# The position bias of the differential pairs: 16-bit products on TensorE, or 32-bit additions on VectorE

## The chip, the cores and the metric

The kernel runs on one core of a Trainium2 chip. A core has TensorE (PE; matmuls, results to PSUM), VectorE (DVE), ScalarE (ACT), GpSimd (POOL) and SyncE (SP, which here only issues DMAs). Each engine takes its instructions strictly in the order in which the program lists them, and waits between engines are waits on counting semaphores. The metric is the time of one execution on the device in microseconds; for the kernel before, three runs took 2700.38, 2700.81 and 2706.25 us, median 2700.81 us.

## The reference

One layer of a hybrid encoder: a joint projection, eight forgetting-attention (FoX) heads, four differential heads, gates and an output projection. The change concerns the differential heads of the prompt (2048 tokens), cut to this:

```python
def diff_block(qp, q):
    s = jnp.einsum('bqhmd,bkhmd->bhmqk', q.astype(f32), kd) * SCALE      # m: two maps per head
    bias = table[t5_bucket(kpos[None, :] - qp[:, None])]
    s = s + jnp.transpose(bias, (2, 0, 1))[None, :, None]
    mask = (kpos[None, :] // CHUNK) <= (qp[:, None] // CHUNK)            # CHUNK = 64
    s = jnp.where(mask, s, NEG_INF)
    p = jax.nn.softmax(s, axis=-1)
    a = p[:, :, 0] - lam * p[:, :, 1]
    return jnp.einsum('bhqk,bkhe->bqhe', a, vd)
```

The bias depends on the distance of key and query alone and is constant from a distance of 128 on. Less that constant, which the softmax doesn't see, and with the mask put in, it differs from zero only in a band two key tiles wide beside the diagonal. The kernel keeps that band as a table of 128 x 256 per head, in two layouts (queries or keys along the partitions).

## The kernel before

Three parts follow each other: the projection of 2176 token columns with the attention of the sample rows woven in (to about 1400 us), the prompt's attention (to 2293 us), and the merge with the output projection. The prompt's attention (`prompt_attention`) goes over eight pairs: pair 0, 2, 4, 6 are two FoX heads each, pair 1, 3, 5, 7 are the two maps of a differential head. A pair has four blocks Q of 512 queries.

There are two passes. **Pass A** finds, for every query, the maximum of its scores and (differential pairs) the sum of the exponentials. A unit of it is one query tile of 128 against up to 1024 keys: TensorE writes the scores to one of two PSUM tiles `sa` (`scores_a`), VectorE takes the maximum (L1913), and for a differential pair ScalarE takes exponentials and their sum (L1861) before TensorE may write the unit after next. **Pass B** has 40 units per pair, one key tile against the 512 queries of a block: for each of two maps TensorE writes scores to `sb` (`scores_b`, one PSUM bank per map), ScalarE takes the exponential into `e` (L1891), VectorE combines the two maps into `w` (L1956; in FoX pairs it sums them up instead, L1972 and L1975), and TensorE multiplies by the values (`product`, L2070 or L2073). TensorE may not write the scores of the next unit to a bank before ScalarE has read this one's.

The bias enters by matmuls. In the projection part VectorE splits the 32-bit table into three bfloat16 parts (event B3, L728 to L738), and in both passes three matmuls of an identity with these parts (L2020 in pass A, L2047 in pass B) stand between the two score matmuls of a banded unit, in the same accumulation. Of pass B the key tiles 4Q-1 to 4Q+3 of a block are banded; of pass A one unit of most tiles.

The order of all this is one list of events written by `events()`; every engine walks it and emits its part. Around each unit u of pass B the list has B(u), E(u), W(u-1), R(u-2), then as many units of pass A (of the pair after, some nine units of pass B ahead) as a work target asks for, then the products V. So pass A of a differential pair runs mainly beside pass B of a FoX pair, and partly beside its own pass B.

## Time and profile before

| What | Value |
|---|---|
| median of three runs | 2700.81 us |
| the profiled execution | 2701.99 us, of which the span from first to last instruction is 2700.3 us |
| busy share of the span | PE 97%, PE weight loads 78%, DVE 49%, ACT 35%, POOL 14% |
| chain that ended last | PE 87%, ACT 4%, DVE 4%, issue 2%, DMA 2%, SPq 1%, POOL 1% |
| granted TensorE clock | 0.994 of full speed |

A row of a group names the line, the engine, the operation, the tiles and shapes, how many there are, the busy time with the mean length of one, and the idle time ahead of them with what ended it. Matmuls overlap in the records: a matmul's length runs from its start to the end of its results, and the next one starts before that, so what a matmul takes from the stream is read from one start to the next.

### The profile page before, as it was taken

To read this page: it belongs to the slowest core of one execution; us is meant where nothing else is said; L and a number is where in the kernel's file an instruction comes from. 1 tells how busy PE (TensorE), PEld (TensorE's weight loads), DVE (VectorE), ACT (ScalarE), POOL (GpSimd) and SP (SyncE) were. 2 spreads that over 40 slices of the span, in tenths; PEclk is the share of its full clock that TensorE was granted. 3 is DMA by queue.
4 is the path that set the end of the run, shared out by engine and by line. 5 is a ranking of instruction groups with operands and counts; after the bars stand their busy time and mean duration, and the time that the engine had idled before them with its cause. 6 is when DMAs were issued, how large, how long until landed. Compare 5 with 4: busy or idle time off the path is not lost.

```text
span 2700.3 us, 37170 instructions
## 1 busy us (share of the span) xinstructions
PE 2616.4 (97%) x14833; PEld 2100.3 (78%) x14833; DVE 1314.2 (49%) x1952; ACT 943.7 (35%) x1837; POOL 391.4 (14%) x398
## 2 busy tenths in 40 slices
PE   7999999999999999999999999999999999999998
PEld 5788888888999999999975565565566556888887
DVE  5321124314443332443347677667667766655553
ACT  4123321112222222100115655664664566422221
POOL 1100001131100000012244103212211330200000
PEclk9999999999999999999989999999999999999999
DMA  4543334448786676675843235054151422544432
GB/s 136 164 130 109 109 108 134 135 146 223 213 213 188 177 192 181 184 195 154 218 133 69 50 78 127 5 126 100 32 122 37 99 67 82 182 135 133 136 120 96
DMA packets 405772, 353.67 MB, mean 131 GB/s; under 512 B 45440, under 2 KB 368968, under 8 KB 399416
## 3 DMA queue, kind: packets, MB, share of 16 engines
q1 hardware_dynamic: 396464, 332.66, 45.6%
q0 software_dynamic: 9136, 18.63, 2.1%
...
## 4 chain that ended last, share of the span: by engine, by line
PE 87%; ACT 4%; DVE 4%; issue 2%; DMA 2%; SPq 1%; POOL 1%; ACTq 0%; DVEq 0%; POOLq 0%
PE p_acc L851 14%; PE p_acc L856 13%; PE p_acc L855 13%; PE a_op L2073 5%; PE a_sb L2042 4%; PE a_sb L2049 4%; PE a_op L2070 4%; PE a_sa L2018 3%; PE a_sa L2023 2%; PE e_U L1410 2%; PE a_sa L2021 2%; PE p_turn L885 2%; PE e_U L1411 2%; PE e_U L1412 2%; ACT a_e L1891 1%
## 5 line engine op out<-in xcount | busy, mean ns | idle before, releaser
L851 PE MATMUL p_acc<-p_h_hi,p_w_hi 128*128 128x384 f32 (+1 forms) x1960 | 718.0, 366 | 1.4 <-DVE p_h_lo L667 1.4
L856 PE MATMUL p_acc<-p_h_hi,p_w_lo 128*128 128x384 f32 (+1 forms) x1920 | 687.1, 358 | 0.0
L855 PE MATMUL p_acc<-p_h_lo,p_w_hi 128*128 128x384 f32 (+1 forms) x1920 | 686.5, 358 | 0.0
L1913 DVE TENSOR_REDUCE a_nmax<-a_sa 128x1 f32<-128x1024 f32 (+7 forms) x384 | 347.7, 910 | 282.2 <-PE a_sa L2021 166.7
L1891 ACT ACTIVATE a_e<-a_sb 128x512 f32<-128x512 f32 (+3 forms) x640 | 315.7, 534 | 313.7 <-PE a_sb L2049 311.2
L851 PEld LDWEIGHTS p_acc<-p_h_hi,p_w_hi 128*128 128x128 f32 x1960 | 369.7, 189 | 35.8 <-issue 4.0
L856 PEld LDWEIGHTS p_acc<-p_h_hi,p_w_lo 128*128 128x128 f32 x1920 | 361.0, 188 | 30.5
L855 PEld LDWEIGHTS p_acc<-p_h_lo,p_w_hi 128*128 128x128 f32 x1920 | 361.8, 188 | 28.7
L2042 PE MATMUL a_sb<-a_q,a_k 128*128 128x512 f32 (+2 forms) x640 | 276.5, 434 | 9.1 <-ACT a_e L1891 8.9
L2049 PE MATMUL a_sb<-a_q,a_k 68*128 68x512 f32 (+2 forms) x640 | 247.7, 389 | 0.0
L653 DVE TENSOR_TENSOR p_w_lo<-p_raw,p_w_hi 128x1024 fp32r<-128x1024 f32 x96 | 129.2, 1346 | 220.4 <-ACT p_w_hi L584 220.4
L564 POOL TENSOR_SCALAR p_ev_hi<-p_ev 128x896 fp32r<-128x896 f32 (+1 forms) x32 | 33.7, 1052 | 1234.3 <-DVE p_ev L551 1004.2
L584 ACT CAST p_w_hi<-p_raw 128x1024 fp32r<-128x1024 f32 x98 | 102.4, 1045 | 300.3 <-PE p_acc L856 254.6
L2042 PEld LDWEIGHTS a_sb<-a_q,a_k 128*128 128x128 f32 x640 | 122.7, 192 | 79.9 <-issue 35.0
L1861 ACT ACTIVATE a_sa<-a_sa,a_nmax 128x1024 f32<-128x1024 f32 (+4 forms) x192 | 162.6, 847 | 34.6 <-DVE a_nmax L1913 34.4
L551 DVE COPY p_ev<-p_acc 128x384 f32<-128x384 f32 (+1 forms) x80 | 48.8, 610 | 226.3 <-PE p_acc L856 226.3
L544 ACT ACTIVATE p_ev<-p_acc 128x384 f32<-128x384 f32 (+1 forms) x80 | 42.7, 534 | 298.9 <-PE p_acc L856 298.5
L2018 PE MATMUL a_sa<-a_k,a_q 128*128 128x512 f32 (+4 forms) x320 | 125.9, 394 | 20.6 <-ACT a_sa L1861 20.6
L2070 PE MATMUL a_op<-a_w,a_v 128*128 128x512 f32 (+3 forms) x320 | 144.8, 534 | 0.4
L2073 PE MATMUL a_op<-a_e,a_v 128*64 128x512 f32 (+3 forms) x640 | 139.0, 546 | 2.9 <-issue 2.9
L1975 DVE TENSOR_TENSOR a_run<-a_run,a_e 128x1024 f32<-128x1024 f32 (+3 forms) x128 | 137.4, 1074 | 1.4 <-DVE a_run L1975 0.5
L2049 PEld LDWEIGHTS a_sb<-a_q,a_k 68*128 68x128 f32 x640 | 122.5, 191 | 17.7 <-issue 5.5
...
## 6 DMA issues: line engine op xcount, KB each, us to landing
...
```

Of the source, the lines that this page charges most:

```text
L851: nc.tensor.matmul(acc[a % 2][:, 0:n], hi, h_hi[p][:, k, at:at + n], start=(k == 0), stop=False)
L855: nc.tensor.matmul(acc[a % 2][:, 0:n], hi, h_lo[p][:, k, at:at + n], start=False, stop=False)
L856: last = nc.tensor.matmul(acc[a % 2][:, 0:n], lo, h_hi[p][:, k, at:at + n], start=False, stop=(k == DK - 1))
L1861: nc.scalar.activation(scores_of(ev[1]), scores_of(ev[1]), ACT.Exp, bias=nmax[:, b % 2, c, col:col + 1], accum_out=total[:, b % 2, c, col: ...
L1891: nc.scalar.activation(e[:, u % E_SLOTS, m, cols], sb_[m][:, cols], ACT.Exp).then_inc(e_made, 1)
L1913: nc.vector.tensor_reduce(nmax[:, b % 2, c, col:col + 1], scores_of(ev[1]), axes, ALU.max, negate=True).then_inc(a_maxed, 1)
L1975: nc.vector.tensor_tensor(sum_, sum_, now, ALU.add).then_inc(e_added, 1)
L2018: nc.tensor.matmul(out, q1[z][m][:, qs], k1[z][m][:, k0:k0 + wide], start=True, stop=False)
L2042: nc.tensor.matmul(out, k1[z][m][:, ks], q1[z][m][:, qs], start=True, stop=False)
L2049: nc.tensor.matmul(out, k2[z][m][0:ROW_C + 2, ks], q2[z][m][0:ROW_C + 2, qs], start=False, stop=True).then_inc(b_scored, 1)
L2070: last = nc.tensor.matmul(op[:, cols], v[z][:, kt, :], w[:, u % W_SLOTS, cols], start=(kt == 0), stop=final)
L2073: last = nc.tensor.matmul(op[m * HD:(m + 1) * HD, cols], v[z][:, kt, m * HD:(m + 1) * HD], e[:, u % E_SLOTS, m, cols], start=(kt == 0), st ...
```

## The change

The three 16-bit parts go, with the VectorE work that makes them, and the band tables stay 32-bit. TensorE issues no bias matmuls any more. In pass A VectorE adds the table to the banded 128 or 256 columns of the scores in PSUM and then, waiting for its own addition (`a_biased`), takes the maximum. In pass B VectorE adds it to each map's scores in PSUM (`b_biased`); ScalarE's exponential of a banded unit waits for that addition instead of for TensorE. The addition stands at the event E(u), ahead of W(u-1) and of the maxima that follow it in the list. The table of a pair comes in two DMAs of 128 KB instead of six of 64 KB. The core of the diff:

```diff
@@ the projection part
-        for i in range(3):
-            at(10 + i, 0, ("B3", i))
+        at(10, 0, ("B3",))
@@ SyncE, B3
                 for y in range(2):
-                    sp.dma_start(d["band"][y, :, i].rearrange("h p n -> p h n"), part[i][:, y]).then_inc(band_stored, 16)
+                    sp.dma_start(d["band"][y].rearrange("h p n -> p h n"), band[:, y]).then_inc(band_stored, 16)
@@ VectorE, B3: the two memsets of the mask stay
-                    nc.vector.tensor_copy(part[0][:], band[:]).then_inc(band_step, 1)
-                    nc.vector.tensor_tensor(rest, band[:], part[0][:], ALU.subtract).then_inc(band_step, 1)
-                    nc.vector.tensor_copy(part[1][:], rest).then_inc(band_step, 1)
-                    nc.vector.tensor_tensor(rest, rest, part[1][:], ALU.subtract).then_inc(band_step, 1)
-                    nc.vector.tensor_copy(part[2][:], rest).then_inc(band_step, 1)
@@ prompt_attention
-        band = s.sb("band", [P, 2, 3, BAND], BF16)
+        band = s.sb("band", [P, 2, BAND])
+    def banded(a):
+        b, m, t, c = a
+        tile = 4 * (b % BLOCKS) + t
+        first = max((tile - 1) * P, c * CHUNK_KEYS)
+        end = c * CHUNK_KEYS + a_width(a)
+        return (end - first, first - (tile - 1) * P) if is_diff(b) and first < end else None
+    in_band = lambda b, kt: is_diff(b) and kt >= 4 * (b % BLOCKS) - 1
@@ ScalarE, E
-                    act.wait_ge(b_scored, 2 * u + m + 1)
+                    if in_band(*B_UNITS[u]):
+                        act.wait_ge(b_biased, 2 * n_band[u] + m + 1)
+                    else:
+                        act.wait_ge(b_scored, 2 * u + m + 1)
@@ VectorE, A
+                if banded(A_UNITS[ev[1]]):
+                    n, at = banded(A_UNITS[ev[1]])
+                    if (m, c) == (0, 0):
+                        dve.wait_ge(side_in[1], side_total(b // BLOCKS))
+                    b0, n_b = banks(a_width(A_UNITS[ev[1]]))[-1]
+                    end = n_b + (512 if b0 else 0)
+                    square = sa[ev[1] % 2][:, end - n:end]
+                    nc.vector.tensor_tensor(square, square, band[:, 0, at:at + n], ALU.add).then_inc(a_biased, 1)
+                    dve.wait_ge(a_biased, n_biased[ev[1] + 1])
@@ VectorE, E
+            elif ev[0] == "E" and in_band(*B_UNITS[ev[1]]):
+                u = ev[1]
+                t0 = B_UNITS[u][1] - 4 * (B_UNITS[u][0] % BLOCKS)
+                lo, hi = max(t0, 0) * P, min(t0 + 2, 4) * P
+                if t0 <= 0:
+                    dve.wait_ge(side_in[1], side_total(B_UNITS[u][0] // BLOCKS))
+                for m in range(MAPS):
+                    dve.wait_ge(b_scored, 2 * u + m + 1)
+                    nc.vector.tensor_tensor(sb_[m][:, lo:hi], sb_[m][:, lo:hi], band[:, 1, lo - t0 * P:hi - t0 * P],
+                                            ALU.add).then_inc(b_biased, 1)
@@ TensorE, scores_a
-                    for cols, msk in adds:
-                        nc.tensor.matmul(out[:, cols], ident16[:], msk, start=False, stop=False)
@@ TensorE, scores_b
-                if is_diff(b) and kt >= 4 * Q - 1:
-                    t0 = kt - 4 * Q
-                    lo, hi = max(t0, 0) * P, min(t0 + 2, 4) * P
-                    for n in range(3):
-                        nc.tensor.matmul(sb_[m][:, lo:hi], ident16[:], band[:, 1, n, lo - t0 * P:hi - t0 * P],
-                                         start=False, stop=False)
```

What moves on VectorE in pass B, at the end of the last block of pair 3 (about 1844 to 1853 us of the profile): `a_w` is the combined map, `a_nmax` the maximum of a pass A unit. Before:

```order
L1913 TENSOR_REDUCE a_nmax<-a_sa 128x1 [waits a_a_scored] x2
L1956 SCALAR_TENSOR_TENSOR a_w<-a_e,a_lam 128x512 [waits a_multiplied,a_e_made]
L1913 TENSOR_REDUCE a_nmax<-a_sa 128x1 [waits a_a_scored]
L1956 SCALAR_TENSOR_TENSOR a_w<-a_e,a_lam 128x512 [waits a_multiplied,a_e_made]
L1913 TENSOR_REDUCE a_nmax<-a_sa 128x1 [waits a_a_scored]
L1956 SCALAR_TENSOR_TENSOR a_w<-a_e,a_lam 128x384 [waits a_multiplied,a_e_made]
L1913 TENSOR_REDUCE a_nmax<-a_sa 128x1 [waits a_a_scored] x2
```

The same place in the changed kernel (its L1918 is L1913 of before, L1971 is L1956):

```order
L1918 TENSOR_REDUCE a_nmax<-a_sa 128x1 [waits a_a_scored] x2
L1964 TENSOR_TENSOR a_sb<-a_sb,a_band 128x256 [waits a_b_scored,a_side_in1]
L1964 TENSOR_TENSOR a_sb<-a_sb,a_band 128x256 [waits a_b_scored]
L1971 SCALAR_TENSOR_TENSOR a_w<-a_e,a_lam 128x512 [waits a_multiplied,a_e_made]
L1918 TENSOR_REDUCE a_nmax<-a_sa 128x1 [waits a_a_scored]
L1964 TENSOR_TENSOR a_sb<-a_sb,a_band 128x256 [waits a_b_scored] x2
L1971 SCALAR_TENSOR_TENSOR a_w<-a_e,a_lam 128x512 [waits a_multiplied,a_e_made]
L1918 TENSOR_REDUCE a_nmax<-a_sa 128x1 [waits a_a_scored]
L1964 TENSOR_TENSOR a_sb<-a_sb,a_band 128x256 [waits a_b_scored] x2
L1971 SCALAR_TENSOR_TENSOR a_w<-a_e,a_lam 128x384 [waits a_multiplied,a_e_made]
L1918 TENSOR_REDUCE a_nmax<-a_sa 128x1 [waits a_a_scored] x2
```

Two additions, each waiting for TensorE's scores of its map, now stand behind the maximum and ahead of the combination at every banded unit. What moves on VectorE in pass A of pair 3, beside pass B of pair 2 (`a_run` is the FoX sum, `a_const`, `a_c_hi` and `a_c_lo` close a block). Before:

```order
L1942 TENSOR_TENSOR a_const<-a_nmax,a_log_sum 128x8 [waits a_c_turned,a_f_act]
L1913 TENSOR_REDUCE a_nmax<-a_sa 128x1 [waits a_a_scored] x2
L1975 TENSOR_TENSOR a_run<-a_run,a_e 128x2x384 [waits a_e_added,a_e_masked,a_e_made]
L1948 CAST a_c_hi<-a_cT 8x128 [waits a_c_in1,a_c_turned]
L1950 TENSOR_TENSOR a_c_lo<-a_cT,a_c_hi 8x128 [waits a_f_dve]
L1913 TENSOR_REDUCE a_nmax<-a_sa 128x1 [waits a_a_scored]
L1975 TENSOR_TENSOR a_run<-a_run,a_e 128x2x256 [waits a_e_added,a_e_masked,a_e_made]
```

And after:

```order
L1947 TENSOR_TENSOR a_const<-a_nmax,a_log_sum 128x8 [waits a_c_turned,a_f_act]
L1915 TENSOR_TENSOR a_sa<-a_sa,a_band 128x256 [waits a_a_scored]
L1918 TENSOR_REDUCE a_nmax<-a_sa 128x1 [waits a_a_biased]
L1915 TENSOR_TENSOR a_sa<-a_sa,a_band 128x256 [waits a_side_in1,a_a_scored]
L1918 TENSOR_REDUCE a_nmax<-a_sa 128x1 [waits a_a_biased]
L1990 TENSOR_TENSOR a_run<-a_run,a_e 128x2x384 [waits a_e_added,a_e_masked,a_e_made]
L1953 CAST a_c_hi<-a_cT 8x128 [waits a_c_in1,a_c_turned]
L1955 TENSOR_TENSOR a_c_lo<-a_cT,a_c_hi 8x128 [waits a_f_dve]
L1915 TENSOR_TENSOR a_sa<-a_sa,a_band 128x256 [waits a_a_scored]
L1918 TENSOR_REDUCE a_nmax<-a_sa 128x1 [waits a_a_biased]
L1990 TENSOR_TENSOR a_run<-a_run,a_e 128x2x256 [waits a_e_added,a_e_masked,a_e_made]
```

Each banded maximum has an addition ahead of it, and waits for that addition; the order of everything else is as it was. On TensorE only the triples are gone.

## Rows read from the trace of the kernel before

**Rows 1.** The page: busy time, share of the span and instructions of each engine.

```profile
PE 2616.4 (97%) x14833; PEld 2100.3 (78%) x14833; DVE 1314.2 (49%) x1952; ACT 943.7 (35%) x1837; POOL 391.4 (14%) x398
```

**Rows 2.** Busy time by stretch: pass B of pair 2, of pair 3.

```profile
core 0: us, PE busy (x) PEld busy (x) DVE busy (x) ACT busy (x) POOL busy (x), PEclk, DMA share, GB/s
1633.00:1745.00 112.00, 105.86 (x523) 60.69 (x521) 80.96 (x95) 66.06 (x150) 35.77 (x43) 1.00 0.35 79
1745.00:1857.00 112.00, 109.76 (x552) 73.38 (x551) 75.96 (x120) 62.77 (x128) 13.56 (x22) 1.00 0.34 77
```

**Rows 3.** Groups by shape, 1350 to 2500 us: widest maximum, bias matmuls.

```profile
L1913 DVE TENSOR_REDUCE a_nmax<-a_sa 128x1 f32<-128x1024 f32 x160 | 195.6, 1223 | 146.0 <-PE a_sa L2021 82.3 <-PE a_sa L2023 51.4 <-PE a_sa L2025 12.2
...
L2020 PE MATMUL a_sa<-a_band,a_ident 128*128 128x256 bf16 x336 | 56.2, 276 | 0.0
L2047 PE MATMUL a_sb<-a_band,a_ident 128*128 128x256 bf16 x288 | 48.1, 276 | 0.0
L2047 PE MATMUL a_sb<-a_band,a_ident 128*128 128x128 bf16 x168 | 19.1, 223 | 0.0
...
L2020 PE MATMUL a_sa<-a_band,a_ident 128*128 128x128 bf16 x72 | 8.2, 223 | 0.0
```

**Rows 4.** Timeline of PE (start, length): map 1 without band, to the next start.

```profile
1600.63 0.40 PE L2042 MATMUL a_sb<-a_q,a_k 128*128 128x512 f32 x1
...
1601.10 1.02 PE L2070 MATMUL a_op<-a_w,a_v 128*128 128x512 f32 x2
```

**Rows 5.** Timeline of PE: map 1 of two banded units, to the next start.

```profile
1840.96 0.40 PE L2042 MATMUL a_sb<-a_q,a_k 128*128 128x512 f32 x1
...
1841.67 0.33 PE L2023 MATMUL a_sa<-a_k,a_q 66*128 66x384 f32 x1
...
1844.11 0.39 PE L2042 MATMUL a_sb<-a_q,a_k 128*128 128x512 f32 x1
...
1844.91 0.33 PE L2023 MATMUL a_sa<-a_k,a_q 66*128 66x384 f32 x1
```

**Rows 6.** Groups by shape, VectorE, whole span: the nearest operations.

```profile
L1913 DVE TENSOR_REDUCE a_nmax<-a_sa 128x1 f32<-128x256 f32 x32 | 13.0, 418 | 12.5 <-PE a_sa L2021 6.7 <-PE a_sa L2025 5.5
L1913 DVE TENSOR_REDUCE a_nmax<-a_sa 128x1 f32<-128x128 f32 x32 | 9.0, 286 | 15.5 <-PE a_sa L2021 9.8 <-PE a_sa L2025 5.6
...
L1343 DVE TENSOR_TENSOR e_pair<-e_pair,e_U 128x256 f32<-128x256 f32 x8 | 3.4, 421 | 9.9 <-PE e_U L1412 5.3 <-DMA e_pair<-scratch_gT 3.0 <-issue 1.5
```

**Rows 7.** Timeline of DVE: two maxima in a row, of 128 and of 256.

```profile
1575.14 0.54 DVE L1913 TENSOR_REDUCE a_nmax<-a_sa 128x1 f32<-128x128 f32 x2 [1.39 <-PE a_sa L2025]
...
1577.53 0.76 DVE L1913 TENSOR_REDUCE a_nmax<-a_sa 128x1 f32<-128x256 f32 x2 [0.46 <-PE a_sa L2025]
```

**Rows 8.** Busy time by stretch: the banded units of pair 3, blocks 3, 2, 1, 0.

```profile
1840.00:1853.00 13.00, 13.00 (x74) 8.04 (x73) 8.70 (x12) 4.61 (x10) 0.00 (x0) 1.00 0.00 0
1801.00:1814.00 13.00, 13.00 (x77) 8.05 (x75) 7.76 (x15) 4.26 (x9) 2.05 (x4) 1.00 0.01 2
1768.00:1783.00 15.00, 15.00 (x84) 9.90 (x82) 8.79 (x11) 9.41 (x18) 0.00 (x0) 1.00 1.02 213
1745.00:1759.00 14.00, 12.26 (x76) 7.92 (x75) 7.49 (x15) 8.90 (x21) 2.88 (x3) 1.00 0.01 2
```

**Rows 9.** Busy time by stretch: where VectorE is packed densest.

```profile
1649.00:1665.00 16.00, 15.22 (x77) 8.22 (x75) 13.98 (x15) 8.39 (x19) 4.58 (x6) 1.00 1.02 213
```

**Rows 10.** Waits, 1350 to 2600 us: total, times, longest.

```profile
PEld a_sa L2018 <- ACT a_sa L1861: 49.5, 60, 1.4
...
ACT a_sa L1861 <- DVE a_nmax L1913: 34.4, 44, 2.3
```

**Rows 11.** Busy time by stretch: where TensorE's granted clock is below full.

```profile
1390.00:1400.00 10.00, 6.54 (x18) 3.77 (x18) 7.10 (x10) 1.23 (x3) 5.29 (x4) 0.60 0.37 140
1400.00:1410.00 10.00, 7.10 (x24) 5.34 (x26) 5.04 (x8) 2.30 (x6) 9.42 (x9) 0.50 0.96 214
```

**Rows 12.** Busy time by stretch: projection, while B3 runs.

```profile
150.00:165.00 15.00, 15.00 (x68) 12.43 (x67) 5.41 (x6) 3.67 (x5) 0.00 (x0) 1.00 0.62 171
```

53 lines of the change are left out of this document (18 added, 35 removed).

## The prediction

> **What bounds the kernel now.** I read the page first: TensorE is busy 97% of the span, VectorE 49%, ScalarE 35% [rows 1]. A mean says little here, because the kernel has three parts, so I then cut the time into stretches. In the attention, pass B of a FoX pair and pass B of a differential pair alternate, 112 us each; pairs 2 and 3 stand for the others. In both TensorE is busy nearly throughout (105.9 and 109.8 of 112 us), while VectorE is busy 81.0 and 76.0 of 112 us [rows 2]: 72% and 68%, not 49%. So TensorE bounds both, and VectorE has some 31 to 36 us to spare in each. The groups by shape give what the change removes, the timelines what one piece of it takes, and the waits where a unit already hangs on another engine.
>
> **What it takes from TensorE.** 336 + 72 bias matmuls in pass A and 288 + 168 in pass B [rows 3]: 112 triples of 256 columns and 24 of 128 in pass A, 96 and 56 in pass B. Their busy time is 56.2 + 8.2 + 48.1 + 19.1 = 131.6 us [rows 3], but records overlap, so I measure from start to start. One map without a band takes 1601.10 - 1600.63 = 0.47 us [rows 4]. With a triple of 256 it takes 1844.91 - 1844.11 = 0.80, with one of 128 1841.67 - 1840.96 = 0.71 us [rows 5]. A triple is worth 0.33 or 0.24 us. Pass A: 112 x 0.33 + 24 x 0.24 = 42.7 us. Pass B: 96 x 0.33 + 56 x 0.24 = 45.1 us. Together 87.8 us, if TensorE alone decided.
>
> The Trainium skill says in "Perfetto Trace Analysis", section "Identifying the Most-Contended Engine", that busy time of matmuls is no good measure, since they are pipelined. By the busy column one would expect 131.6 us; the trace agrees with the rule, since the starts leave 87.8 of them.
>
> **What it adds to VectorE.** 136 additions in pass A, 152 in pass B, 208 of 256 columns and 80 of 128. The trace has no addition that reads and writes PSUM. The nearest are an addition of 256 columns with one operand in PSUM, 0.421 us, and the maxima over PSUM of 256 and 128 columns, 0.418 and 0.286 us [rows 6]. Two maxima in a row take 0.76 and 0.54 us together [rows 7], so the second adds only 0.34 or 0.25 us. I take these as what an addition takes from VectorE where nothing waits for it, and 0.42 (0.29) plus 0.03 for the hand-over as what it puts into a chain. The lower end is the same 0.34. For the upper end I let a write to PSUM double the length, 0.84 us: nothing in the rows speaks for that, and it is the end of the range, not the value.
>
> **Pass B, by stretch.** A stretch is the four or five banded units that end a block. The four of pair 3 last 14, 15, 13 and 13 us with VectorE busy 7.5, 8.8, 7.8 and 8.7 us [rows 8]. Block 0 has 6 triples of 256 and 2 of 128, 2.5 us of TensorE and, as additions, 6 x 0.34 + 2 x 0.25 = 2.5 us of VectorE. The others have 6 and 4, 2.9 and 3.0 us. TensorE would need 11.5, 12.1, 10.1 and 10.1 us, VectorE 10.0, 11.8, 10.8 and 11.7. So TensorE still decides in blocks 0 and 1, and VectorE takes over in blocks 2 and 3. Were VectorE packed without a gap, the stretches would take 11.5, 12.1, 10.8 and 11.7 us: 2.5 + 2.9 + 2.2 + 1.3 = 8.9 us per pair, 35.6 us over four pairs. It won't be. Its order is fixed and it waits for each map's scores, with the combination and the maxima behind it. The densest stretch in the trace has it busy 13.98 of 16 us, 87% [rows 9]. At 87% they would take 11.5, 13.6, 12.4 and 13.4 us: 2.5 + 1.4 + 0.6 - 0.4 = 4.1 us per pair, 16.4 us in all. I take the middle, 26 us of the 45.1.
>
> Beside it stands a rule that speaks against the change. The Trainium skill ("Perfetto Trace Analysis", "Optimizing Scalar/DVE Operations") gives VectorE an overhead of about 125 ns per instruction on PSUM. With 128 more columns costing 0.418 - 0.286 = 0.132 us, 256 columns are 0.264 us, and an estimate by that page is 0.39 us of engine time instead of 0.34. That adds 0.4 us to each stretch that VectorE bounds and takes some 3 us from the 26. The two maxima in a row are PSUM reads and cost 0.34 [rows 7], so the trace does not bear it out for reads; for a write to PSUM no row decides.
>
> **Pass A.** VectorE has room here: pass A of a differential pair lies mostly beside pass B of a FoX pair, 81.0 us busy of 112 [rows 2], and 25 additions of about 0.4 make it 91 of about 104. What matters is the loop of one `sa` tile: scores, addition, maximum, exponential, and only then the scores of the unit after next. The loop loses a triple (-0.33) and gains an addition with its hand-over (+0.45): +0.12 us. Where TensorE sets the pace the triple is a gain; where the loop does, it becomes +0.12, 0.45 us less than that. TensorE's weight load waits for this exponential 60 times, and the exponential itself waits for the maximum 44 times in all [rows 10]. In the others ScalarE was busy with pass B exponentials, which cover the addition. I count the 44: 42.7 - 44 x 0.45 = 22.9 us. The ends are 42.7 us (all covered) and, with all 136 on the loop, -136 x 0.12 = -16 us.
>
> **Edits at nothing.** The splitting of the table and its stores go, in a stretch where TensorE is busy 15.00 of 15 us [rows 12]: it hides them, and nothing is gained. Four stores and sixteen loads of the table fewer are no term: their issue on SyncE stands beside hundreds of others, and no wait of rows 10 is on them. ScalarE keeps its instructions; its exponential of a banded unit comes later by an addition and earlier by the triples ahead of its scores, 0.42 against 0.33 for map 0.
>
> **Sum.** 26 + 22.9 = 49 us, taken from the profiled execution's 2701.99 us (its span and 1.7 us around it, 1.2 us over the median): 2653 us.
>
> **Rivals.**
> 1. *TensorE stays the bound, VectorE hides everything.* For it: the 31 to 36 us to spare per stretch of 112 [rows 2], against about 10 us of additions in a FoX stretch and 15 in a differential one. Against it: blocks 2 and 3 [rows 8], where demand exceeds TensorE's. Time 2701.99 - 87.8 = 2614 us; whatever ends below 2635 I count here.
> 2. *The gain is lost to hand-overs.* Pass B gives its 16 us, pass A nothing, or the additions run long: at 0.84 us, 0.5 us more each, a stretch of blocks 2 and 3 grows by 5 us and eats that up. Time 2685 to 2706 us.
> 3. *Slower: the addition queues behind a maximum.* A maximum of 1024 columns takes 1.22 us [rows 3], and VectorE is strictly in order, so map 0's scores lie until it ends, ScalarE's exponential and TensorE's next scores behind them. At half a maximum plus the addition, 0.6 + 0.34, all 76 banded units could wait up to 0.95 us. It decides from 45.1 / 76 = 0.59 us of TensorE wait per unit. At the full 0.95 pass B turns from -45 to +27 us, and with pass A at nothing the time is 2729 us. For it: the order puts the maxima directly ahead of the additions. Against it: TensorE has a pass A unit's scores and a product, whose two matmuls alone are 1.02 us long [rows 4], to do in between, and two `sa` tiles of lead.
> 4. *The clock.* Where TensorE was busy only 6.5 and 7.1 of 10 us, the granted clock was 0.60 and 0.50, that is partly and wholly at 1.2 of its 2.4 GHz [rows 11]; in all stretches of rows 2 and 8 it was full. With VectorE as bound TensorE would be busy about 10.1 of 12.4 us, 81%, well above. If it fell in the eight stretches of blocks 2 and 3, each would need 10.1 us more: 80 us, 2734 us.
>
> **How the numbers follow.** The forecast (2635 to 2680) 0.52, rival 1 0.20, rival 2 0.17, rival 3 0.09, rival 4 0.02. A change under 0.2%, 5.4 us, can't be told from none: 2695.4 to 2706.2 us. Of rival 2 I put 0.09 on faster, 0.06 on the same, 0.02 on slower. Faster 0.52 + 0.20 + 0.09 = 0.81, same 0.06, slower 0.02 + 0.09 + 0.02 = 0.13. The range leaves out the complete cover, below 2620, and what lies above 2702: 2620 to 2702 us.
>
> **What the profile will show.** PE loses 864 matmuls, and the FoX and differential stretches fall from 112 us, together by about 12 us per pair of pairs: more by far than that means rival 1, and less rival 2. Additions in PSUM should read 0.42 and 0.29 us; 0.6 or more would break the sum in pass B first. In blocks 2 and 3 of pair 3 VectorE should be busy over 85% and TensorE wait for ScalarE's exponential, in blocks 0 and 1 not. In pass A ScalarE's waits for a maximum should become more than 44. The forecast is wrong if the exponential of banded units starts more than 0.6 us later after its scores than an addition takes, unit after unit, or if the clock falls anywhere past 1420 us.

## The result: a third of the gain that was forecast

| | before | after |
|---|---|---|
| median | 2700.86 us (4 runs, 2700.38 to 2706.25) | 2683.68 us (4 runs, 2682.77 to 2686.19) |
| ratio | | 0.993, 95% interval 0.9918 to 0.9943 |
| profiled execution / span | 2701.99 / 2700.3 us | 2683.03 / 2681.3 us |
| granted TensorE clock | 0.994 | 0.986 |

The change gains 17 us, and the forecast was 49 (2653 us). The sign and the range (2620 to 2702 us) held, the size did not.

### The profile page after: what moved, and what is told of

Same layout as the page of the kernel before. It is cut to its first block, busy times and chain, and to the rows that moved or that the text cites. A ratio compares the mean times of both kernels' runs of the same rounds, so it can differ in the third digit from the quotient of the medians.

```text
span 2681.3 us, 35769 instructions
## 1 busy us (share of the span) xinstructions
PE 2560.4 (95%) x13969; PEld 2055.5 (77%) x13969; DVE 1396.2 (52%) x2235; ACT 939.4 (35%) x1837; POOL 392.6 (15%) x398
## 4 chain that ended last, share of the span: by engine, by line
PE 81%; DVE 7%; ACT 5%; issue 3%; DMA 2%; SPq 1%; POOL 1%; DVEq 0%; ACTq 0%; POOLq 0%
PE p_acc L832 14%; PE p_acc L837 14%; PE p_acc L836 14%; PE a_op L2074 5%; PE a_sb L2049 4%; PE a_sb L2050 3%; PE a_op L2071 3%; PE a_sa L2027 2%; PE a_sa L2030 2%; PE e_U L1391 2%; PE p_turn L866 2%; PE e_U L1392 2%; PE e_U L1393 2%; ACT a_e L1887 2%; PE a_sa L2028 2%
## 5 line engine op out<-in xcount | busy, mean ns | idle before, releaser
L1918 DVE TENSOR_REDUCE a_nmax<-a_sa 128x1 f32<-128x1024 f32 (+7 forms) x384 | 347.0, 910 | 130.1 <-PE a_sa L2032 43.9
L1887 ACT ACTIVATE a_e<-a_sb 128x512 f32<-128x512 f32 (+3 forms) x640 | 310.6, 533 | 281.7 <-PE a_sb L2050 185.2
L2049 PE MATMUL a_sb<-a_q,a_k 128*128 128x512 f32 (+2 forms) x640 | 277.0, 436 | 21.1 <-ACT a_e L1887 18.1
L2050 PE MATMUL a_sb<-a_q,a_k 68*128 68x512 f32 (+2 forms) x640 | 237.5, 374 | 0.0
L2049 PEld LDWEIGHTS a_sb<-a_q,a_k 128*128 128x128 f32 x640 | 124.3, 194 | 109.3 <-ACT a_e L1887 52.1
L579 ACT CAST p_w_hi<-p_raw 128x1024 fp32r<-128x1024 f32 x98 | 102.4, 1045 | 300.0 <-PE p_acc L837 241.6
L1854 ACT ACTIVATE a_sa<-a_sa,a_nmax 128x1024 f32<-128x1024 f32 (+4 forms) x192 | 162.3, 846 | 50.8 <-DVE a_nmax L1918 49.6
L2027 PE MATMUL a_sa<-a_k,a_q 128*128 128x512 f32 (+4 forms) x320 | 132.0, 414 | 41.0 <-ACT a_sa L1854 40.9
L539 ACT ACTIVATE p_ev<-p_acc 128x384 f32<-128x384 f32 (+1 forms) x80 | 42.7, 534 | 298.5 <-PE p_acc L837 298.1
L2074 PE MATMUL a_op<-a_e,a_v 128*64 128x512 f32 (+3 forms) x640 | 144.5, 565 | 2.9 <-issue 2.9
L2050 PEld LDWEIGHTS a_sb<-a_q,a_k 68*128 68x128 f32 x640 | 124.7, 195 | 23.2 <-issue 10.1
L1990 DVE TENSOR_TENSOR a_run<-a_run,a_e 128x1024 f32<-128x1024 f32 (+3 forms) x128 | 137.1, 1071 | 0.6
```

The source lines that it names most:

```text
L1854: nc.scalar.activation(scores_of(ev[1]), scores_of(ev[1]), ACT.Exp, bias=nmax[:, b % 2, c, col:col + 1], accum_out=total[:, b % 2, c, col: ...
L1887: nc.scalar.activation(e[:, u % E_SLOTS, m, cols], sb_[m][:, cols], ACT.Exp).then_inc(e_made, 1)
L1918: nc.vector.tensor_reduce(nmax[:, b % 2, c, col:col + 1], scores_of(ev[1]), axes, ALU.max, negate=True).then_inc(a_maxed, 1)
L1990: nc.vector.tensor_tensor(sum_, sum_, now, ALU.add).then_inc(e_added, 1)
L2027: nc.tensor.matmul(out, q1[z][m][:, qs], k1[z][m][:, k0:k0 + wide], start=True, stop=False)
L2049: nc.tensor.matmul(out, k1[z][m][:, ks], q1[z][m][:, qs], start=True, stop=False)
```

## The profile after

The page after, answering [rows 1]: busy time, share of the span and instructions of each engine.

```profile
PE 2560.4 (95%) x13969; PEld 2055.5 (77%) x13969; DVE 1396.2 (52%) x2235; ACT 939.4 (35%) x1837; POOL 392.6 (15%) x398
```

The 864 matmuls are gone, VectorE has 283 instructions and 82 us more. Pass B of pair 2 and of pair 3 after, answering [rows 2]:

```profile
core 0: us, PE busy (x) PEld busy (x) DVE busy (x) ACT busy (x) POOL busy (x), PEclk, DMA share, GB/s
1627.50:1737.50 110.00, 100.63 (x441) 55.86 (x439) 88.40 (x119) 65.56 (x148) 35.40 (x42) 0.97 0.36 80
1737.50:1841.50 104.00, 95.91 (x391) 63.16 (x390) 87.58 (x163) 59.39 (x124) 12.99 (x20) 0.98 0.37 82
```

TensorE now stands idle 9.4 and 8.1 us in them, against 6.1 and 2.2 before, and its clock is no longer full. VectorE is at 80% and 84%, so over the whole stretch its busy time bounds neither. How long the stretches are is read best from the products of the differential pairs, by their line: durations (min, median, max) and first and last start, in pair 1, pair 3 and pair 7. Before:

```profile
L2070 PE MATMUL a_op<-a_w,a_v x80: 272/591/667, 1531.9 to 1632.2; 128*128 128x512 f32 x56, 128*128 128x384 f32 x8, 128*128 128x256 f32 x8, 128*128 128x128 f32 x8
L2070 PE MATMUL a_op<-a_w,a_v x80: 272/590/667, 1756.1 to 1856.3; 128*128 128x512 f32 x56, 128*128 128x384 f32 x8, 128*128 128x256 f32 x8, 128*128 128x128 f32 x8
L2070 PE MATMUL a_op<-a_w,a_v x80: 272/590/594, 2204.2 to 2292.6; 128*128 128x512 f32 x56, 128*128 128x384 f32 x8, 128*128 128x256 f32 x8, 128*128 128x128 f32 x8
```

And after:

```profile
L2071 PE MATMUL a_op<-a_w,a_v x80: 272/592/668, 1530.5 to 1625.5; 128*128 128x512 f32 x56, 128*128 128x384 f32 x8, 128*128 128x256 f32 x8, 128*128 128x128 f32 x8
L2071 PE MATMUL a_op<-a_w,a_v x80: 272/592/1191, 1749.2 to 1844.5; 128*128 128x512 f32 x56, 128*128 128x384 f32 x8, 128*128 128x256 f32 x8, 128*128 128x128 f32 x8
L2071 PE MATMUL a_op<-a_w,a_v x80: 272/590/1055, 2186.1 to 2274.3; 128*128 128x512 f32 x56, 128*128 128x384 f32 x8, 128*128 128x256 f32 x8, 128*128 128x128 f32 x8
```

From pair 1 to pair 3 a pair of pairs takes 218.7 us instead of 224.2; 12 us less was forecast (the same distance from pair 3 to 5 and from pair 5 to 7 shrank by 3.9 and 7.3 us). The differential part of pair 3 (first to last product) went from 100.2 to 95.3 us, the part ahead of it, from the last differential product of pair 1 on, below called a FoX stretch, from 123.9 to 123.7. Some 8 of the 10.7 us of TensorE work that pass A loses per pair lay there, and no gain is to be seen. The stretch also holds most of block 0 of the differential pair: its scores begin at 1737.7, its first product at 1749.2.

The last differential part, pair 7, gained nothing worth the name: 88.4 us before, 88.2 after, where pairs 1, 3 and 5 gained 5.3, 4.9 and 5.5. The longest pause of TensorE there is before block 3, for a DMA that brings the row constants made from pass A's maxima:

```profile
2241.40 0.50 PE L2049 MATMUL a_sb<-a_q,a_k 128*128 128x512 f32 x1 [2.75 <-DMA a_q<-a_c_lo]
```

In the trace of before TensorE's matmuls don't wait for this DMA at all; one weight load does, for 0.7 us.

The additions and the widest maximum by shape (after; the maximum is L1918 now), answering [rows 3, 6]:

```profile
L1918 DVE TENSOR_REDUCE a_nmax<-a_sa 128x1 f32<-128x1024 f32 x160 | 195.4, 1222 | 93.7 <-PE a_sa L2030 42.8 <-PE a_sa L2028 37.5 <-PE a_sa L2032 12.2
L1915 DVE TENSOR_TENSOR a_sa<-a_sa,a_band 128x256 f32<-128x256 f32 x112 | 47.7, 426 | 34.1 <-PE a_sa L2028 33.6
L1964 DVE TENSOR_TENSOR a_sb<-a_sb,a_band 128x256 f32<-128x256 f32 x96 | 37.5, 424 | 6.5 <-PE a_sb L2050 6.1
L1964 DVE TENSOR_TENSOR a_sb<-a_sb,a_band 128x128 f32<-128x128 f32 x56 | 14.9, 292 | 4.0 <-PE a_sb L2050 2.3
```

The price of an addition that reads and writes PSUM was forecast well: 0.42 and 0.29 us, and the double length at the end of the range did not come. The waits, answering [rows 10]. Before, beside the weight loads of those rows, the matmuls themselves waited this long:

```profile
PE a_sa L2018 <- ACT a_sa L1861: 20.6, 36, 1.2
```

After; exponentials are L1854 in pass A, L1887 in pass B, scores L2027 and L2049:

```profile
ACT a_e L1887 <- DVE a_sb L1964: 94.7, 72, 3.7
PEld a_sa L2027 <- ACT a_sa L1854: 76.3, 83, 2.3
PEld a_sb L2049 <- ACT a_e L1887: 52.1, 123, 1.8
ACT a_sa L1854 <- DVE a_nmax L1918: 49.6, 53, 2.4
PE a_sa L2027 <- ACT a_sa L1854: 40.9, 49, 1.9
```

TensorE's weight load waits for the pass A exponential 83 times and 76.3 us, against 60 times and 49.5 us, and the matmul 40.9 us against 20.6; the exponential for its maximum 53 times against 44. So a good part of the time went into the loop of the `sa` tile, and it is ScalarE's exponential that TensorE waits for.

How such a pause comes about, in pass B of pair 2: VectorE's timeline (start, length, idle time before), then ScalarE's, then TensorE's.

```profile
1708.52 1.22 DVE L1918 TENSOR_REDUCE a_nmax<-a_sa 128x1 f32<-128x1024 f32 x1
```

```profile
1707.77 0.19 ACT L1854 ACTIVATION_READ_ACCUMULATOR a_sa<-a_sa,a_nmax 128x1 f32 x1
1710.37 1.08 ACT L1887 ACTIVATE a_e<-a_sb 128x512 f32<-128x512 f32 x2 [2.40 <-PE a_sb L2050]
1711.34 1.10 ACT L1854 ACTIVATE a_sa<-a_sa,a_nmax 128x1024 f32<-128x1024 f32 x1
```

```profile
1710.64 0.29 PE L2027 MATMUL a_sa<-a_k,a_q 128*128 128x256 f32 x1
...
1712.60 0.50 PE L2027 MATMUL a_sa<-a_k,a_q 128*128 128x512 f32 x1 [1.55 <-ACT a_sa L1854]
...
1714.02 0.63 PE L2049 MATMUL a_sb<-a_q,a_k 128*128 128x512 f32 x1
1714.44 0.63 PE L2050 MATMUL a_sb<-a_q,a_k 68*128 68x512 f32 x1
...
1716.28 3.68 PE L2074 MATMUL a_op<-a_e,a_v 128*64 128x512 f32 x8
...
1719.90 0.52 PE L2049 MATMUL a_sb<-a_q,a_k 128*128 128x512 f32 x1
```

VectorE ended the maximum of this 1024-wide unit at 1708.52 + 1.22 = 1709.74. ScalarE, idle, did not take its exponential then: in its order two pass B exponentials stand ahead, whose scores came at 1710.4. So it began at 1711.34, ended at 1712.4, and TensorE stood 1.55 us. Then a second cost shows: matmuls of 512 columns start 0.42 us apart (1714.02, 1714.44) instead of 0.23. The granted clock fell to 1.2 GHz (0.66 as a mean of 1710 to 1720 us, shown below). The same place of pair 6 had the same pause without the fall:

```profile
2151.24 0.50 PE L2027 MATMUL a_sa<-a_k,a_q 128*128 128x512 f32 x1 [1.55 <-ACT a_sa L1854]
...
2152.29 0.39 PE L2049 MATMUL a_sb<-a_q,a_k 128*128 128x512 f32 x1
2152.52 0.40 PE L2050 MATMUL a_sb<-a_q,a_k 68*128 68x512 f32 x1
...
2153.55 1.94 PE L2074 MATMUL a_op<-a_e,a_v 128*64 128x512 f32 x8
2155.42 0.50 PE L2049 MATMUL a_sb<-a_q,a_k 128*128 128x512 f32 x1
```

From scores to the next scores it is 1719.90 - 1714.02 = 5.88 us there and 2155.42 - 2152.29 = 3.13 us here: 2.75 us from this fall in one unit. Three of the stretches with such falls, answering [rows 11]; past 1420 us the trace of before had none in the attention:

```profile
core 0: us, PE busy (x) PEld busy (x) DVE busy (x) ACT busy (x) POOL busy (x), PEclk, DMA share, GB/s
1710.00:1720.00 10.00, 8.45 (x25) 4.37 (x23) 5.99 (x8) 4.93 (x10) 0.00 (x0) 0.66 0.00 0
1740.00:1750.00 10.00, 6.62 (x29) 4.52 (x30) 6.00 (x15) 6.16 (x15) 0.86 (x1) 0.86 0.00 1
2180.00:2190.00 10.00, 8.91 (x34) 5.40 (x31) 5.77 (x13) 5.93 (x14) 3.85 (x4) 0.62 0.00 1
```

The trace has seven falls in the attention. The pause of TensorE last before each was 1.1, 1.6, 2.1, 1.6, 1.9, 1.9 and 2.75 us long; the last one is the wait for the DMA of pair 7. Of the other six, three lie in FoX pairs and three in block 0 of pairs 3, 5 and 7.

The four banded stretches of pair 3, from the start of the first unit's scores to the start of the next stretch (forecast at 87% packing and in full):

| us | block 0 | block 1 | block 2 | block 3 |
|---|---|---|---|---|
| before | 15.70 | 17.12 | 13.86 | 13.11 |
| after | 16.23 | 15.06 | 11.47 | 12.37 |
| gain | -0.53 | 2.06 | 2.39 | 0.74 |
| forecast gain | 2.5 | 1.4 to 2.9 | 0.6 to 2.2 | -0.4 to 1.3 |

Blocks 1 to 3 came as forecast. VectorE is busy 11.26 of 11.47 us in block 2 and 11.84 of 12.37 in block 3, 98% and 96%: it is the bound there, as the forecast had it, and packed closer than the 87% of its lower end. Block 0, where I let TensorE decide, got slower. VectorE there, after:

```profile
1742.48 1.23 DVE L1918 TENSOR_REDUCE a_nmax<-a_sa 128x1 f32<-128x1024 f32 x1 [1.45 <-PE a_sa L2028]
...
1743.98 0.76 DVE L1964 TENSOR_TENSOR a_sb<-a_sb,a_band 128x256 f32<-128x256 f32 x2
1744.64 0.74 DVE L1971 SCALAR_TENSOR_TENSOR a_w<-a_e,a_lam 128x512 f32<-128x512 f32 x1
1745.30 0.42 DVE L1990 TENSOR_TENSOR a_run<-a_run,a_e 128x256 f32<-128x256 f32 x1
```

And TensorE beside it:

```profile
1743.07 0.65 PE L2074 MATMUL a_op<-a_e,a_v 128*64 128x256 f32 x4
1745.87 1.08 PE L2099 MATMUL a_cT<-a_run,a_ones 128*64 128x512 f32 x4 [2.14 <-DVE a_gap L1932]
```

Block 0 of a differential pair is where the FoX pair ahead of it is closed. The matmul that totals that pair's sums (L2099) needs its last sum (L1990), and on VectorE this stands behind a maximum, two additions and a combination: TensorE waits 2.14 us, against 0.78 before. The releaser named, L1932, comes right behind the sum. Some 4.6 us earlier in the same block TensorE waits for a pass A exponential, 1.87 us against 0.96 before.

The row of two additions at 1743.98 also settles what I left open beside the Trainium skill ("Perfetto Trace Analysis", "Optimizing Scalar/DVE Operations"): two take 0.76 us, so the second adds 0.34 us, as two maxima did. The estimate of 0.39 us from that page's overhead on PSUM is not borne out for a write to PSUM either.

## The experiments

The kernel before took 2701 to 2702 us beside every group of them, so differences of a microsecond or two between groups mean nothing. Low time below is 2 x (1 - granted clock) x span: the kernel before has 32 us (0.994), the changed one 75 us (0.986).

**One pass each.** In `b_only` VectorE adds in pass B and TensorE keeps pass A's triples; `a_only` is the reverse. The edit of `b_only` against the changed kernel:

```diff
@@ VectorE, A
-                    nc.vector.tensor_tensor(square, square, band[:, 0, at:at + n], ALU.add).then_inc(a_biased, 1)
@@ TensorE, scores_a
+                        adds += [(slice(at, at + n_m), band[:, n, c0:c0 + n_m]) for n in range(3)]
```

> The additions of pass B alone; pass A keeps its three 16-bit bias matmuls as before. Theory 1 (the loop of an sa tile in the FoX stretches is what eats the gain, and TensorE's pauses there pull its clock down): FoX stretches as before (about 123.8 us from one differential product stretch to the next), differential stretches keep their 5 us gain (95 instead of 100 us), mean granted clock back to 0.994, time about 2680 us, no slower than the full change. Theory 2 (VectorE is simply too full, either pass costs its share): half of the 17 us, about 2692 us.

> The additions of pass A alone; pass B keeps its bias matmuls. Theory 1: nothing gained or a loss, 2698 to 2708 us, with a mean granted clock below 0.994 and the FoX stretches no shorter than 123.8 us. Theory 2: the other half of the gain, about 2692 us, clock 0.994.

`b_only` took 2689.05 us (ratio 0.9954, 0.9942 to 0.9967; clock 0.990), `a_only` 2686.91 us (0.9950, 0.9937 to 0.9962; clock 0.992). Pass B is worth 13.1 us, pass A 15.3, and both together not 28.4 but 17 to 18. Both first theories missed. `b_only` should have given all of the gain at a full clock; it gave three quarters at 0.990, its differential parts in pairs 1, 3 and 5 gained 5.7 us each as expected, and its FoX stretches grew from 123.8 to 124.3 and 125.3 us. `a_only` should have given nothing (2698 to 2708 us, FoX stretches no shorter than 123.8); it gained, with FoX stretches of 120.0 to 122.2 us. So pass A's additions alone don't eat what its triples give back. In the full change something takes it away again in the same stretches. The additions of block 0 lie there; `block0` below tests them.

**The FoX sum later.** A first guess was that maxima stand behind the 1.2 us FoX sum. `r_later` puts the sum behind them:

```diff
-            if u >= 2:
-                out.append(("R", u - 2))
             share = pass_a(target(u))
             if not finish:
                 next(share, None)
             stages(1)
+            if u >= 2:
+                out.append(("R", u - 2))
```

> The full change, with the FoX sum (1.2 us on VectorE) moved behind the pass A maximum of its iteration instead of ahead of it. Theory 1: the loop loses up to 1.2 us where it binds, FoX stretches shrink by 3 to 8 us each, clock nearer 0.994, time 2655 to 2672 us. Theory 2: the same work in another order, 2680 to 2688 us.

2710.46 us (1.0040, 1.0026 to 1.0054; clock 0.983), 27 us slower than the changed kernel, where 12 to 29 us faster was expected; FoX stretches of 130 us. The guess fell. The matmul of the totals (L2099) now waits for this sum 16 times, 25.2 us in all, against 7.2 us in 4 waits in the changed kernel, while TensorE's wait for the pass A exponential is as it was (40.7 against 40.9 us). What comes late at a block's end is this sum.

**ScalarE's order.** `x_early` lets each pass A exponential stand ahead of the next iteration's pass B exponentials, in the changed kernel; `x_early_before` does so in the kernel before.

```diff
                 out.append(("A", done))
-                if done > a_first[b]:
-                    out.append(("X", done - 1))
+                out.append(("X", done))
```

> The full change, with ScalarE's order altered: each exponential of pass A stands right behind the scores of its own unit, ahead of the pass B exponentials of the next iteration, and no longer behind them. Theory Q (queueing on ScalarE: a ready pass A exponential, which frees TensorE's score tile, waits behind pass B exponentials that are not ready): the FoX stretches of the differential passes shrink from 124.8 to about 121 us each, block 0 from 16.2 to 15.5 us, fewer falls of the clock, total about 2665 us. Theory V (VectorE itself is too late, whatever ScalarE's order): within 3 us of 2684. Third outcome: pass B exponentials now stand behind pass A ones that are late, and the time rises to 2690 or more.

> The same alteration of ScalarE's order in the kernel before. Theory Q: before, TensorE's own work covered most of the queueing, so the gain is smaller than in the changed kernel, 0 to 8 us (2694 to 2702). If it gains as much as the changed kernel does, the queueing has nothing to do with the change.

2704.71 us (1.0005, 0.9988 to 1.0022) and 2710.28 us (1.0031, 1.0019 to 1.0043): the third outcome in the changed kernel, and a loss, which neither theory had, in the kernel before. The trace of `x_early` shows both sides: TensorE's wait for the pass A exponential falls from 40.9 to 10.7 us, so the queue on ScalarE is real, but ScalarE waits for maxima 155 times and 163.2 us (before this edit 53 times and 49.6), and TensorE for the pass B exponential 56.8 us instead of 18.1. The order that stood was the better one, by 21 and 9 us.

**Pricing the parts of pass A.** `a_zeros` keeps the additions and leaves TensorE its triples, on a tile of zeros:

```diff
@@ TensorE, scores_a
+                        adds += [(slice(at, at + n_m), zeros[:, 0:n_m]) for n in range(3)]
```

> The full change, but TensorE keeps pass A's three 16-bit products for each pair of squares, with zeros in place of the bias parts; VectorE adds the bias as in the change. It prices the additions of pass A at unchanged TensorE work (against the kernel with pass B's additions alone, 2689 us) and the removal by itself (against the changed kernel, 2684 us). Theory of the loop (the addition lengthens the loop of the score tile, and TensorE's work sat beside it): additions cost 5 to 15 us, removal gains 10 to 20, so 2694 to 2704 us, with fewer falls of the clock than in the changed kernel. Rival, additive costs (TensorE bound throughout, additions delay by themselves): additions 35 us, removal 40: about 2724 us.

2697.94 us (0.9984, 0.9975 to 0.9992). Against `b_only` the additions cost 8.9 us; against the changed kernel the removal gains 14.3 us, not 42.7. Both lie where the loop theory had them.

**Block 0 of pass B back to TensorE.** The 16-bit parts of the table for pass B come back with it (their making in the projection part, three stores, and three DMAs of 64 KB per pair).

```diff
-    in_band = lambda b, kt: is_diff(b) and kt >= 4 * (b % BLOCKS) - 1
+    in_band = lambda b, kt: is_diff(b) and b % BLOCKS > 0 and kt >= 4 * (b % BLOCKS) - 1
@@ TensorE, scores_b
+                if is_diff(b) and Q == 0:
+                    lo, hi = kt * P, min(kt + 2, 4) * P
+                    for n in range(3):
+                        nc.tensor.matmul(sb_[m][:, lo:hi], ident16[:], band16[:, n, lo - kt * P:hi - kt * P],
+                                         start=False, stop=False)
```

> The full change, except that pass B's block 0 of each differential pair keeps its three 16-bit products on TensorE (blocks 1 to 3 and pass A go by VectorE). Theory Q/loop: in block 0 all four units are banded, VectorE's additions come one behind another and hold up ScalarE's queue, so block 0 loses with them: pair 3's block 0 falls from 16.2 to about 15.5 us and the following unit pays less for the clock, total 2676 to 2682 us. Rival (block 0 is slow from the start of pair loads and turns, not from the additions): block 0 at 16.5 or more, total 2684 to 2690 us.

2673.34 us (0.9891, 0.9878 to 0.9904; clock 0.991), 10 us below the changed kernel and better than expected. Block 0 of pair 3 takes 15.33 us, the other stretches are as in the changed kernel within 0.02 us, and the same matmul of the totals waits as little as before the change:

```profile
1740.53 0.65 PE L2104 MATMUL a_op<-a_e,a_v 128*64 128x256 f32 x4
1741.96 1.08 PE L2129 MATMUL a_cT<-a_run,a_ones 128*64 128x512 f32 x4 [0.77 <-DVE a_gap L1957]
```

The low time falls from 75 to 48 us with it. By the count of the section on the clock that alone would be 11 us, so these 10 us can't be divided between a shorter block 0 and fewer falls behind it.

The next four start from this kernel. In `a_wide` units of up to 512 columns keep TensorE's triples; in `one_col` the addition of pass A takes one column (most of the bias is left out there); in `sum_part` the FoX sums off the diagonal take one map of two; `step_500` changes one number of the planner, and `step_800` took it further in the following group.

```diff
@@ a_wide
+            ... and a_width(a) > 512 else None
@@ one_col
-                    nc.vector.tensor_tensor(square, square, band[:, 0, at:at + n], ALU.add).then_inc(a_biased, 1)
+                    nc.vector.tensor_tensor(square[:, 0:1], square[:, 0:1], band[:, 0, at:at + 1], ALU.add).then_inc(a_biased, 1)
@@ sum_part
+                    part = slice(0, 2 if on_edge(b, kt) else 1)
+                    nc.vector.tensor_tensor(sum_[:, part], sum_[:, part], now[:, part], ALU.add).then_inc(e_added, 1)
@@ step_500
-    STEP = 300
+    STEP = 500
```

> As the kernel whose block 0 of pass B stays with TensorE (2673 us), and in pass A TensorE also keeps its three 16-bit products in units of up to 512 columns; VectorE adds the bias in the wider ones only. Theory of the loop (two score tiles take turns; scores, addition, maximum, exponential stand one behind another, and in narrow units TensorE waits for that anyway): the products of narrow units cost nothing beside the wait, and the addition taken out shortens the loop: 2664 to 2672 us. Rival (TensorE's work decides in narrow units too): 64 units times about 0.25 us come back, 2683 to 2690 us.

> As the kernel whose block 0 of pass B stays with TensorE (2673 us), but pass A's additions take one column instead of up to 256: most of the bias is left out of the row maxima and sums, and the hand-over stays. If it is the length of the addition that delays the maximum: about 0.25 us shorter in each of 384 units, of which some 200 stand on a wait, so 2625 to 2650 us and fewer waits of TensorE for the pass A exponential. If it is the extra hand-over (addition ends, maximum starts) or something else: within 10 us of 2673.

> As the kernel whose block 0 of pass B stays with TensorE (2673 us), but the FoX passes' running sums on VectorE take one of the two maps in all units that aren't on the diagonal: half of their columns are left out. Theory V (VectorE's queue: pass A's additions and maxima stand behind the sums of 1.2 us): the FoX stretches of 121 us shorten by 2 to 4 us each, total 2655 to 2666 us. Theory of the loop (the chain score, addition, maximum, exponential itself, whatever else VectorE does): within 4 us of 2673.

> As the kernel whose block 0 of pass B stays with TensorE (2673 us), with the planner's fixed cost of one pass A unit at 500 columns in place of 300, so that narrow units are spread over more iterations and wide ones over fewer. Theory of the loop: a unit's fixed part (hand-overs, now with the addition) counts for more than the plan holds, so 2662 to 2672 us. Rival (the spread was right as it stood, wide units now bunch up): 2675 to 2685 us.

> As the kernel with 500 columns (2664 us), with 800. Theory of the loop: units count almost alike, so that the pauses spread further: 2656 to 2664 us. Rival (wide units bunch up in the iterations that have them): 2668 to 2680 us.

| | median us | ratio (95%) |
|---|---|---|
| `a_wide` | 2676.57 | 0.9907 (0.9892 to 0.9922) |
| `one_col` | 2667.23 | 0.9881 (0.9862 to 0.9900) |
| `sum_part` | 2673.24 | 0.9892 (0.9877 to 0.9907) |
| `step_500` | 2663.64 | 0.9863 (0.9845 to 0.9880) |
| `step_800` | 2664.44 | 0.9865 (0.9850 to 0.9880) |

(The expectation of `one_col` counts 384 units; the differential pairs have 192, of which 136 get an addition. The same slip stands in `short_exp`.) The length of pass A's additions is worth 6 us (the second outcome), half of the off-diagonal FoX sums nothing: how much VectorE has to do beside a FoX pair is not the limit. `a_wide` came between its two theories: 48 x 0.33 + 16 x 0.24 = 20 us of TensorE work back, with 64 additions less, cost 3 us, so the products are neither free nor of full price. Spreading the units otherwise gains 9 to 10 us, with both numbers. Their intervals (up to 0.9880) still touch that of `block0` (from 0.9878), so the size is known poorly.

**No bias at all.** `none_a` (from the block 0 kernel) leaves pass A's bias out, `none_both` (from the changed kernel) that of both passes: neither products nor additions. `step_500_before` has the planner's number in the kernel before.

```diff
@@ none_a, none_both
-                    nc.vector.tensor_tensor(square, square, band[:, 0, at:at + n], ALU.add).then_inc(a_biased, 1)
-                    dve.wait_ge(a_biased, n_biased[ev[1] + 1])
@@ none_both
-                    nc.vector.tensor_tensor(sb_[m][:, lo:hi], sb_[m][:, lo:hi], band[:, 1, lo - t0 * P:hi - t0 * P],
-                                            ALU.add).then_inc(b_biased, 1)
```

> As the kernel whose block 0 of pass B stays with TensorE (2673 us), but pass A's bias is left out altogether: no addition and no product. Theory L (removed TensorE work in pass A is worth little whatever replaces it, since the chain score, maximum, exponential of two score tiles decides): 2655 to 2667 us, near the 2667 us of one column. Theory H (the second instruction on VectorE and its wait take the gain, even one column of it): 2635 to 2650 us, some 25 us below it.

> The changed kernel with the bias left out in both passes: neither products nor additions. It gives the worth of the 87.8 us of TensorE work by itself, the ceiling of the change. Theory L: 45 to 60 us of it come through, 2640 to 2657 us. Theory H: nearly all of it does, 2612 to 2630 us.

> The kernel before with the planner's fixed cost of a pass A unit at 500 columns in place of 300. Theory of the loop: before, TensorE's products covered more of a unit's hand-overs, so the gain is smaller than the 10 us of the changed order: 0 to 5 us (2697 to 2702). If it gains 10 us too, the spread has nothing to do with the change.

`none_a` took 2665.75 us (0.9863, 0.9849 to 0.9877), `none_both` 2650.71 us (0.9814, 0.9801 to 0.9826), `step_500_before` 2702.93 us (1.0005, 0.9997 to 1.0014). This is the main finding: with nothing in place of the products, 50.7 of the 87.8 us come through, 58%. Of the 37 us missing some 13 are the clock (0.988, see below). In the trace of `none_both` the waits for ScalarE are longer than in the kernel before (49.5 and 20.6 us), with no addition in them:

```profile
PEld a_sa L2018 <- ACT a_sa L1854: 62.4, 68, 1.8
...
PE a_sa L2018 <- ACT a_sa L1854: 30.5, 40, 1.6
```

The 58% are a mean over two kinds of stretch. Counted from the records of the kernel before, a FoX stretch holds 27 triples of pass A and 6 of block 0, 10.3 us by the prices of the prediction, and a differential part 32 of pass B and 7 of pass A, 11.6 us. What each gained, by the first and last differential products:

| | triples, us | gain of `none_both` | gain of the change |
|---|---|---|---|
| up to pair 1's first product | 10.3 | 3.3 | 1.4 |
| differential parts 1, 3, 5 | 11.6 each | 11.0, 10.4, 10.1 | 5.3, 4.9, 5.5 |
| FoX stretches to pairs 3, 5, 7 | 10.3 each | 2.9, 4.3, 3.5 | 0.2, -1.0, 1.8 |
| differential part 7 | 11.6 | 6.7 | 0.2 |

In the differential parts of pairs 1, 3 and 5, where TensorE had been busy 109.8 of 112 us (pair 3), nine tenths of the removed work come through; in a FoX stretch, where it had been busy 105.9 and waited for the exponentials already, a third does. Part 7 stands out in both: `none_both` too waits for the DMA of the row constants there, 2.6 us.

The banded stretches of pair 3 in `none_both` take 14.21, 13.40, 10.87 and 10.10 us: the additions of pass B cost 2.0 + 1.7 + 0.6 + 2.3 = 6.6 us in this pair. In pass A they cost 2673.34 - 2665.75 = 7.6 us in all. And the better plan gains nothing before the change. The traces show where it goes: in `step_500_before` the FoX stretches shrink from 123.8 to 120.5 us, and the differential parts, where TensorE was full, grow from 100.2 to 102.4 (pair 7's from 88.4 to 96.4). In `step_500` the FoX stretches shrink as well (120 to 122 us in `block0`, 117 to 120 there), and the differential parts of pairs 1, 3 and 5 stay at 94.6; only pair 7's grows, from 86.8 to 93.8.

**One link of the loop shorter.** In the changed kernel, the pass A exponentials (`short_exp`) or maxima (`short_max`) of differential pairs take the first 128 columns only; the rest of the row sum, or of the maximum, is left out.

```diff
@@ short_exp
-                nc.scalar.activation(scores_of(ev[1]), scores_of(ev[1]), ACT.Exp, ...
+                nc.scalar.activation(first(scores_of(ev[1])), first(scores_of(ev[1])), ACT.Exp, ...
@@ short_max
-                nc.vector.tensor_reduce(nmax[:, b % 2, c, col:col + 1], scores_of(ev[1]),
+                nc.vector.tensor_reduce(nmax[:, b % 2, c, col:col + 1], tile_,
```

> The changed kernel with each pass A exponential of the differential pairs taken over its first 128 columns only (the rest of the row sum is left out). Theory of the loop (score tiles come free when their exponential ends, and ScalarE's queue passes the delay on): about 0.6 us less in the chain of 384 units, the FoX stretches shrink from 124 us by 3 to 6 us each and TensorE's waits for the pass A exponential (76 and 41 us) halve: 2655 to 2668 us. If something else decides (TensorE's own order and work, VectorE): within 5 us of 2684.

> The changed kernel with each pass A maximum of the differential pairs taken over its first 128 columns only (the other columns are left out of the maximum). Theory of the loop: a link on VectorE counts as one on ScalarE does, with VectorE's queue shorter as well: 2655 to 2668 us, like the kernel with short exponentials. If only ScalarE's queue decides: 2675 to 2682 us. If neither: within 5 us of 2684.

`short_exp` took 2647.36 us (0.9800, 0.9786 to 0.9813; clock 0.991), 36 us below the changed kernel and 8 us below the range expected; `short_max` 2668.72 us (0.9876, 0.9862 to 0.9889; clock 0.985), 15 below. TensorE's work is the same in both. In `short_exp`:

```profile
L1855 ACT ACTIVATE a_sa<-a_sa,a_nmax 128x128 f32<-128x128 f32 x192 | 66.4, 346 | 95.0 <-DVE a_nmax L1919 94.6
```

```profile
ACT a_sa L1855 <- DVE a_nmax L1919: 94.6, 87, 2.4
...
PEld a_sa L2028 <- ACT a_sa L1855: 41.1, 53, 1.6
...
PE a_sa L2028 <- ACT a_sa L1855: 18.8, 28, 1.1
```

The waits for the exponential halve (76.3 to 41.1 and 40.9 to 18.8 us), as expected. In `short_max` the maximum lost more than that:

```profile
L1920 DVE TENSOR_REDUCE a_nmax<-a_sa 128x1 f32<-128x128 f32 x208 | 60.3, 290 | 75.3 <-PE a_sa L2030 64.6 <-PE a_sa L2034 5.5
```

A widest maximum went from 1.22 to 0.29 us, a widest exponential from 1.10 to 0.35, and yet the exponential gained more than twice as much. That a link on VectorE counts like one on ScalarE was expected, and missed. Part of the distance is the clock: by the count below, at an equal clock the exponential gains some 25 us and the maximum 16. ScalarE is busy 35% of the span, and its exponential is the dearest link of the loop. A reason that fits, and that no run tests by itself: its end is what TensorE waits for, and pass B's exponentials queue behind it.

## The clock's share

Executions of one kernel differ in the clock that they were granted, and their times with it. Least squares over low time: `x_early`, 12 executions from 75 to 120 us of low time, 0.46 us per us (correlation 0.98); `step_500_before`, 12 from 32 to 60 us, 0.38 (0.99); `r_later`, 8 from 87 to 120 us, 0.44 (0.97); `a_zeros`, 11, only 0.21 (0.86). Kernels with four to six executions scatter from 0.06 to 0.69. I take 0.42. The changed kernel has 43 us more low time than the kernel before: some 18 us. The Trainium skill ("TensorE: Matmul & The Clock Gate", "HAM oscillation — how this bites in real kernels") counts half of the low time as lost; these slopes are a little below that. That work which TensorE waits for anyway loses nothing would explain it, and is not tested. This is a correlation, with 2.75 us for a fall in one unit beside it: no run held the clock while all else stayed, and a longer pause could bring both the time and the fall. By the same count `b_only` and `a_only` lose 9 and 5 us, so at an equal clock they gain 22 and 20 us, and both together 35, nearer to the sum of 42 than 17 is to 28.

## Why the prediction was wrong

- **What bounds the kernel**: the step that failed. I read 105.9 and 109.8 busy of 112 us as TensorE deciding throughout ("So TensorE bounds both"), and let every triple count in full unless an addition was in its way. `none_both` gives 50.7 us for 87.8 with no addition anywhere. The reading held for the differential parts of pairs 1, 3 and 5 (10 to 11 of 11.6 us) and failed for the FoX stretches (3 to 4 of 10.3), where most of pass A's triples are: with a triple taken out, TensorE waits for the exponential of the score tile instead.
- **Addition lengths**: right, 0.42 and 0.29 us, and 0.34 in a row.
- **Pass B, 26 us**: measured 13.1 alone, about 22 at an equal clock. Blocks 1 to 3 of pair 3 right (5.2 us against 1.6 to 6.4), block 0 wrong in sign: 2.5 us forecast, -0.5 measured. I took the triples off the stretch's length and missed that VectorE closes the FoX pair there; the row itself had TensorE idle 1.7 of 14 us [rows 8]. `block0` shows it: 10 us from moving that block alone, falls of the clock included. And I let pair 3 stand for all four: pair 7 gained 0.2 us where the others gained about 5.
- **Pass A, 22.9 us**: 15.3 alone, about 20 at an equal clock. Almost the right number, by luck: two errors that offset each other. The additions cost less than the 44 x 0.45 = 20 us that I took off (8.9 in `a_zeros`, 7.6 by `none_a`), and the removal is worth less than 42.7 (14.3 in `a_zeros`).
- **The clock, rival 4 at 0.02**: the mechanism that I all but excluded, in another place. It did not fall in the banded units of blocks 2 and 3 with VectorE as bound, but after pauses of 1.1 to 2.75 us, in FoX pairs, in block 0 and once behind a DMA. About 18 of the 32 us missing, by the correlation; I had not asked what short pauses do to it. The forecast named a fall past 1420 us as its own refutation.
- **Rival 1** (2614 us) fell with `none_both`. **Rival 2**, the gain lost to hand-overs (2685 to 2706 us), came nearest in time, 1 us below its range; in mechanism it holds for a part only, as `one_col` and `none_a` show. **Rival 3**: exponentials do wait for additions (94.7 us, 72 times, up to 3.7 us), but blocks 1 to 3 gained all the same.
- **Edits at nothing**: right as far as the traces show. The last matmul of the projection starts at 1388.3 us, against 1388.0 before, so nothing is gained up to there. The 1.4 us by which the first differential product is earlier (1530.5 us against 1531.9) were gained behind it, in the FoX pair ahead of pair 1.

What stays open: how the remaining loss divides between the loop and the clock in one and the same pause, and why the row constants of pair 7 come late.
